# Paired attentions: the inverse sums, copied 64 wide, are turned by TensorE, and ScalarE's copies stand between its exponentials

## The reference, cut to what matters

```python
def gqa_attend(q, k, v, bias=None, sink=None):
    s = einsum("bqhgd,bkhd->bhgqk", q, k) * ATTN_SCALE
    if bias is not None: s = s + bias
    if sink is not None:
        p = softmax(concatenate([s, sink_col], axis=-1), axis=-1)[..., :-1]
    else:
        p = softmax(s, axis=-1)
    return einsum("bhgqk,bkhd->bqhgd", p, v)
```

## Time and profile before

| what | value |
|---|---|
| timed runs | 1794.65, 1794.69, 1797.04 us |
| the profiled execution's own time | 1799.19 us |
| its span in the profile | 1797.9 us |
| PE, DVE, ACT, POOL busy | 96%, 55%, 41%, 36% of the span |
| even attention, first scores to last output | about 1138 to 1336 us |
| odd attention, first scores to last output | about 1614 to 1691 us |

### The profile page before, as it was taken

One profiled execution on the slowest core, in us unless ns is written; L12 is line 12 of the kernel. 1 busy time (PEld: TensorE's weight loads), 2 busy tenths in 40 slices (PEclk: granted clock), 3 DMA queues, 4 the chain that ended last, 5 costly groups with the idle time before them and its releaser, 6 DMA issues.

```text
span 1797.9 us, 24836 instructions
## 1 busy us (share of the span) xinstructions
PE 1724.9 (96%) x9530; PEld 1386.2 (77%) x9530; DVE 990.7 (55%) x2000; ACT 742.1 (41%) x1465; POOL 641.6 (36%) x272
## 2 busy tenths in 40 slices
PE   8999999889999999999999999999889999999997
PEld 6889666678888888888788876655568888896776
DVE  4797545533233455555792415566643667975553
ACT  5222344552333454344324432466753225225553
POOL 3877222253334454544646122100003233521132
PEclk9999999999999999999999999999999999999999
DMA  8656221132324233333662221100002442321021
GB/s 236 188 141 188 65 71 48 48 98 80 93 70 141 82 89 99 94 94 99 187 194 88 66 90 36 36 1 1 2 1 59 134 127 74 88 68 47 14 89 53
DMA packets 255155, 156.30 MB, mean 87 GB/s; under 512 B 6017, under 2 KB 250942, under 8 KB 255038
## 3 DMA queue, kind: packets, MB, share of 16 engines
q1 hardware_dynamic: 251518, 147.12, 28.1%
q10 hardware_dynamic: 3520, 7.60, 1.2%
HBM read 152.60 MB, written 2.10 MB: 86 GB/s over the span
## 4 chain that ended last, share of the span: by engine, by line
PE 83%; DVE 7%; issue 4%; ACT 3%; POOL 1%; DMA 1%; ACTq 0%; DVEq 0%; SPq 0%
PE ps L783 66%; PE ps L2417 3%; PE ps L2428 2%; PE ps L2447 2%; POOL w_lo L764 1%; PE ps L1567 1%; DVE mod_sums L1500 1%; PE ps L1551 1%; PE ps L1515 1%; DVE mod_sums_odd L1500 1%; DVE probs L2519 1%; PE ps L789 1%; PE ps L1559 1%; PE ps L2453 1%; PE ps L2165 1%
## 5 line engine op out<-in xcount | busy, mean ns | idle before, releaser
L764 POOL TENSOR_TENSOR w_lo<-w_raw,w_hi 128x1024 fp32r<-128x1024 f32 (+1 forms) x220 | 586.2, 2669 | 1080.9 <-ACT w_hi L705 1080.4
L783 PE MATMUL ps<-h_hi,w_lo 128*128 128x512 f32 x1088 | 433.6, 399 | 10.5 <-DVE h_lo L1102 2.9
L783 PE MATMUL ps<-h_hi,w_hi 128*128 128x512 f32 x1088 | 424.5, 390 | 0.0
L783 PE MATMUL ps<-h_lo,w_hi 128*128 128x512 f32 x1088 | 424.2, 390 | 0.0
L783 PEld LDWEIGHTS ps<-h_hi,w_lo 128*128 128x128 f32 x1088 | 204.5, 188 | 59.8 <-issue 6.0
L705 ACT ACTIVATE w_hi<-w_raw 128x1024 fp32r<-128x1024 f32 (+1 forms) x220 | 228.6, 1044 | 37.1 <-PE ps L783 20.6
L783 PEld LDWEIGHTS ps<-h_hi,w_hi 128*128 128x128 f32 x1088 | 204.3, 188 | 43.7
L783 PEld LDWEIGHTS ps<-h_lo,w_hi 128*128 128x128 f32 x1088 | 204.6, 188 | 41.2 <-issue 1.4
L2502 ACT ACTIVATE probs<-probs,small 128x512 f32<-128x512 f32 (+3 forms) x128 | 93.7, 732 | 24.0 <-DVE small L2519 21.2
L2428 PE MATMUL ps<-ident,probs 128*128 128x128 f32 x528 | 85.8, 287 | 15.2 <-ACT probsT L2485 7.0
L2428 PEld LDWEIGHTS ps<-ident,probs 128*128 128x128 f32 x528 | 56.5, 142 | 54.4 <-issue 30.3
(11 more groups left out here) (425 smaller groups left out, 3313.6 us busy)
## 6 DMA issues: line engine op xcount, KB each, us to landing
w_raw<-in_w_in SPq DMA_DIRECT2D x56, 512.0 KB, 5.2
mod_raw<-in_mod_w SPq DMA_DIRECT2D x24, 1024.0 KB, 5.9
w_raw<-in_w_up SPq DMA_DIRECT2D x44, 512.0 KB, 3.8
w_raw<-in_od_w_in SPq DMA_DIRECT2D x28, 512.0 KB, 3.8
w_raw<-in_ev_w_in SPq DMA_DIRECT2D x20, 512.0 KB, 3.8
w_raw<-in_w_down SPq DMA_DIRECT2D x16, 512.0 KB, 4.3
w_raw<-in_w_mem_kv SPq DMA_DIRECT2D x8, 512.0 KB, 3.9
w_raw<-in_w_attn_branch SPq DMA_DIRECT2D x8, 512.0 KB, 4.0
```

What stands on the lines that cost most here:

```text
L764: POOL.tensor_tensor(wlo[:, p, 0:n], raw[:, p, 0:n], f(whi[:, p, 0:n]), ALU.subtract).then_inc(*chunk_lo.by(c))
L783: ins = PE.matmul(out, l, r, start=first and n == 0, stop=last and n == 2)
```

## The change: what it does

- The inverse sums are no longer spread by four matmuls for each output. VectorE copies the 128x2x2 inverses of an output 64 times over into a new buffer inv_wide (128x2x128, one buffer) in a new function `dve_widen`, once for each output: in steps p = 2g+3, behind the output of that step and ahead of the first head's maximum. It waits for the reciprocal of the output's second pair and for `p_weighted` of the output before. TensorE turns the two 128x128 halves of inv_wide with two transposes in the same place of its order and waits for the new event `p_widened` there.
- VectorE's reciprocal no longer waits for `p_weighted`.
- ScalarE's order in step p is now: first head's copy of pair p-1, first head's exponential of pair p, in even steps p = 2g+4 the inverse of output g, second head's copy of pair p-1, second head's exponential of pair p.
- The events `conv_summed` and `ln_summed` become two events of one semaphore; no instruction is added or removed by it.

```diff
--- before.py
+++ after.py
@@ -189,6 +189,7 @@
     stat = sb("statistics", [P, len(NORMS) + 2, 8])
     rowvec = sb("rowvec", [1, 16])
     djunk = nc.alloc_sbuf_tensor_at("diff_squares", [P, 2, P], F32, offset=base[0])
+    inv_wide = nc.alloc_sbuf_tensor_at("inv_wide", [P, 2, P], F32, offset=base[0])
     lamrow = sb("lamrow", [1, 4, DIFF_DH])
     modT = sb("mod_T", [P, 2, 24, 2])
     R0 = base[0]
@@ -490,6 +491,7 @@
     p_copied_act = signal("p_copied_act", halves)
     p_inverted = signal("p_inverted", pairs)
     p_weighted = signal("p_weighted", outs)
+    p_widened = signal("p_widened", outs)
     p_inv_copied = signal("p_inv_copied", outs)
     p_attended = signal("p_attended", outs)
 
@@ -552,12 +554,11 @@
     g_lo = signal("g_lo", gated + each("cg", 4))
     glu_done = signal("glu_done", range(4))
     convolved = signal("convolved", range(CT))
-    conv_summed = signal("conv_summed", [0])
+    conv_summed = signal("conv_summed", ["values", "squares"])
     mean_set = signal("mean_set", [0])
     centred = signal("centred", range(CT))
     bias_masked = signal("bias_masked", range(8))
     ln_squared = signal("ln_squared", range(CT))
-    ln_summed = signal("ln_summed", [0])
     ln_rms = signal("ln_rms", [0])
     ln_diag = signal("ln_diag", [0])
     ln_spread = signal("ln_spread", [0])
@@ -2446,12 +2447,9 @@
             for s in range(2):
                 PE.matmul(ps[s * HEAD:(s + 1) * HEAD, b * 512 + lo:b * 512 + hi], u0["v"](k, s),
                           probsT[s][g % 2][:, k, lo:hi], start=n == 0, stop=n == len(tiles) - 1, skip_group_check=True)
-        PE.wait_ge(*p_inverted(x_, 2 * g + 1))
+        PE.wait_ge(*p_widened(x_, g))
         for n in range(2):
-            inv = pair_stats(2 * g + n)[2]
-            for s in range(2):
-                ins = PE.matmul(ps[s * HEAD:(s + 1) * HEAD, b * 512 + (2 + n) * P:b * 512 + (3 + n) * P],
-                                inv[:, s:s + 1].to_broadcast([P, HEAD]), ident[:])
+            ins = PE.transpose(bank(b, P, (2 + n) * P), inv_wide[:, n, :], ident[:])
         ins.then_inc(*p_weighted.by(x_, g))
         yield
 
@@ -2486,15 +2484,19 @@
                             ACT.Copy).then_inc(*p_copied_act.by(x_, p, s))
 
         for p in range(n + 3):
-            if p >= 5 and p % 2:
-                act_inverse((p - 5) // 2, x_, us)
             if 1 <= p <= n:
                 copy(p - 1, 0)
+            if p > n and p % 2 == 0:
+                act_inverse((p - 4) // 2, x_, us)
             if p < n:
                 u = us[p]
                 neg_max, total, _, esink = pair_stats(p)
                 before(p)
                 for s in range(2):
+                    if s and p >= 4 and p % 2 == 0:
+                        act_inverse((p - 4) // 2, x_, us)
+                    if s and p:
+                        copy(p - 1, 1)
                     ACTE.wait_ge(*p_maxed(x_, p, s))
                     if p >= 4:
                         ACTE.wait_ge(*p_inverted(x_, p - 4))
@@ -2503,10 +2505,10 @@
                     if "sink" in u:
                         ins = ACTE.activation(esink[:, s:s + 1], u["sink"][s], ACT.Exp, bias=neg_max[:, s:s + 1])
                     ins.then_inc(*p_exped.by(x_, p, s))
-            if 1 <= p <= n:
+            if p == n:
+                act_inverse((p - 4) // 2, x_, us)
                 copy(p - 1, 1)
             yield
-        act_inverse(n // 2 - 1, x_, us)
 
     def dve_maximum(x_, p, u, s, probs):
 
@@ -2534,6 +2536,8 @@
         for p in range(n + 3):
             if p >= 5 and p % 2:
                 dve_out((p - 5) // 2, x_, us)
+            if 3 <= p <= n + 1 and p % 2:
+                dve_widen((p - 3) // 2, x_)
             if p < n:
                 before(p)
                 dve_maximum(x_, p, us[p], 0, probs)
@@ -2542,8 +2546,6 @@
                 u = us[p - 1]
                 _, total, inv, esink = pair_stats(p - 1)
                 DVE.wait_ge(*p_exped(x_, p - 1, 1))
-                if p >= 5:
-                    DVE.wait_ge(*p_weighted(x_, (p - 5) // 2))
                 if "sink" in u:
                     dve_step(DVE.tensor_tensor(total, total, esink, ALU.add))
                     dve_after()
@@ -2554,6 +2556,16 @@
                 copy(p - 1, 1)
             yield
         dve_out(n // 2 - 1, x_, us)
+
+    def dve_widen(g, x_):
+
+        DVE.wait_ge(*p_inverted(x_, 2 * g + 1))
+        if g:
+            DVE.wait_ge(*p_weighted(x_, g - 1))
+        at = 48 + 16 * (g % 2)
+        inv = small[:, at:at + 16].rearrange("p (n e) -> p n e", n=2)[:, :, 4:6]
+        DVE.tensor_copy(inv_wide[:].rearrange("p n (s d) -> p n s d", s=2),
+                        inv.unsqueeze(3).to_broadcast([P, 2, 2, HEAD])).then_inc(*p_widened.by(x_, g))
 
     def dve_out(g, x_, us):
 
@@ -3009,17 +3021,17 @@
             for t in range(CT):
                 PE.wait_ge(*convolved(t))
                 ins = PE.matmul(bank(1), ones[:], yc[:, t, :], start=t == 0, stop=t == CT - 1)
-            ins.then_inc(*conv_summed.by(0))
+            ins.then_inc(*conv_summed.by("values"))
         if p == 9:
             for t in range(CT):
                 PE.wait_ge(*ln_squared(t))
                 for b in range(NB):
                     ins = PE.matmul(bank(3, 1, b), sqc[t][:, b * P:(b + 1) * P], ones[:, 0:1], start=t == 0 and b == 0,
                                     stop=t == CT - 1, skip_group_check=True)
-            ins.then_inc(*ln_summed.by(0))
+            ins.then_inc(*conv_summed.by("squares"))
 
     def act_ln_mean():
-        ACTE.wait_ge(*conv_summed(0))
+        ACTE.wait_ge(*conv_summed("values"))
         ACTE.activation(mean[:], bank(1), ACT.Copy, scale=1.0 / 512).then_inc(*mean_set.by(0))
 
     def dve_ln_centre(t):
@@ -3033,7 +3045,7 @@
 
     def act_ln_root():
         ACTE.preload_act_table(ACT.Sqrt)
-        ACTE.wait_ge(*ln_summed(0))
+        ACTE.wait_ge(*conv_summed("squares"))
         ACTE.activation(statistics("ln")[0], bank(3, NB), ACT.Sqrt, scale=1.0 / 512, bias=eps).then_inc(*ln_rms.by(0))
         ACTE.preload_act_table(ACT.Exp)
 
```

## The result

The changed kernel's median is 1787.26 us (1785.91 to 1788.40, 5 executions), against 1796.99 us of the kernel before in its 5. The ratio is 0.995, with a 95% interval of 0.9935 to 0.9964: it is 6.5 to 11.7 us faster. 1787.26 lies inside the range, but the 14 us of the forecast lie outside the interval. The profiled execution took 1788.40 us, span 1787.1.

What follows compares the result with a forecast made beforehand. PE was taken to bound the kernel (83% of the chain), idling 22.8 us in three attention stretches. Terms 7.7 + 6.8 + 1.6 - 1.5 - 0.5 = 14.1, taken as 14, gave a median of 1780.7 us, range 1776.5 to 1788.

Steps and rivals of the forecast that it cites:

- part 1: PE, all 32 outputs: two transposes replace the four inverse matmuls, saving 0.24 us each, 7.7 us in all.
- part 5: In B, PE's scores wait longer for the second maximum: about half of 12 outputs return their 0.24, 1.5 us.
- the clock as a rival: Two-tile pairs of A and B: transposes make PE's clock fall, 3.4 us each; six falls give 1801 us; chance 0.03.
- Parts 2 and 3: ACT's second copy ahead of its second exponential saves 6.8 us; ACT's inverse one step earlier saves 1.6 in B.
- Part 4: DVE's widening copy, 32 times 0.35 us, 11 us in all, is hidden by the wait for the inverse it replaces.
- The rival of the uncovered copy: DVE's widening copy delays the maxima and costs PE 0.2 us per output, 32 outputs; gain 7.6 us, 1787.1; chance 0.14.
- 0.5 for the start: Steps at each attention's very start run beside the last projections and lack these stalls: 0.5 us off the gain.
- the 4 us that I had named as the mark of an error: Sign of being wrong: PE's wait in B for DVE's maxima (L2519) grows past 4 us.
- the 1.9 forecast for ACT's stalls: In A, PE's 3 waits for ACT's copy, 1.9 us, go; counted within the 6.8 us for ACT's second copy.
- The rival in which everything comes back: ACT's stalls return as waits for DVE's copies and maxima; gain only 2 to 4 us, about 1792; chance 0.07.

Runs made afterwards that it cites:

- the copy alone: Kernel before with only ScalarE's second copy moved ahead of its second exponential; ratio 0.9991, 2.5 us less in the attentions.
- the inverse alone: Kernel before with only ScalarE's copy of the inverse moved from step 2g+5 to 2g+4, between the exponentials; ratio 0.9979, 2.7 us less in the attentions.
- the order alone: Changed kernel with the four inverse matmuls and VectorE's wait for `p_weighted` back, no widening copy, ScalarE's new order kept; ratio 0.9958.

## Why the prediction was right and wrong

The mechanism was the one forecast: the waits for ACT's copy vanished, DVE found its inverse ready in B, the widening copy was hidden, and what was late next was the second maximum. The size was too big by 4 us, 14 against 9.9. It failed in two steps: the gain of the attentions was carried over to the whole program one to one, which left out the clock (2.0 us), and the sum for the attentions was 14.1 where they gave 12.4, mostly in part 1 and in what comes back of it (part 5). Some 0.5 us are left unexplained.

- **What stood outside the sum: the clock, 2.0 us.** I carried the gain in the attentions over to the whole program one to one. I had the clock as a rival only in the two-tile pairs, on the ground of the transposes. There it didn't come: B kept 1.00 in every profile, and A had one fall of 3.4 us near 1155 us before and after alike. The rule of the Trainium skill, "TensorE: Matmul & The Clock Gate", section "Part 4: PE-mode transpose", that transposes don't count as busy for the clock as other matmuls do, is thus not borne out in B, where 176 transposes and 24 new ones changed nothing. It is a test only of turns with scores and values between them. The falls that made the difference were elsewhere; why they come there no run here shows.
- **Part 1, the inverses, 7.7 us: 7.0 by its price, 4.3 in the end.** From the start of the values over the inverses and the turn of six to the next scores it took 1188.38 - 1185.69 = 2.69 us before, and 1190.48 - 1188.01 = 2.47 in the changed kernel. That is 0.22 saved per output, not 0.24. Up to the start of the turn it is only 1.89 - 1.72 = 0.17; the turn itself then takes 0.05 less behind two transposes than behind the four matmuls. I had priced the two as two more in a run; by this count they are 0.02 dearer. The scores of the kernel before, and the stretch of the changed kernel:

```profile
1188.38 0.48 PE L2417 MATMUL ps<-k_A,q_A 64*128 64x256 f32 x1
```

```profile
1188.01 1.51 PE L2448 MATMUL ps<-probsT,v_A 128*64 128x256 f32 x12
1189.46 0.44 PE L2452 MATMUL ps<-ident,inv_wide 128*128 128x128 f32 x2
1189.73 0.82 PE L2429 MATMUL ps<-ident,probs 128*128 128x128 f32 x6
1190.48 0.48 PE L2418 MATMUL ps<-k_A,q_A 64*128 64x256 f32 x1
```

  On top of the new order this part gave 12.4 - 8.1 = 4.3 us, so 2.7 of the 7.0 came back; see part 5. Without the new order it gave nothing in A and came out 1.3 us slower in B.
- **Parts 2 and 3, the order, 6.8 + 1.6: 8.1 together.** Right as a pair, wrong as terms: 2.5 for the copy alone, 2.7 for the inverse alone. So it was partly luck that the two terms added up to nearly the right sum. Each removed wait uncovers the other within a few tenths of a microsecond.
- **Part 4, the copy, 0.35 us and hidden:** the median is 0.28 us (0.31 in the mean, for one copy in the odd attention took 1.04), the next instruction begins 0.20 behind its start, and it is hidden in A and B. Right but for that one: the step that holds it takes 4.27 us, against 3.84 with the order alone. The rival of the uncovered copy, 0.2 us of PE for each of 32, is out.
- **Part 5, what is late next, 1.5 us back, and 0.5 for the start:** 2.7 came back. In seven steps of B that hold an output's inverses nothing of the 0.22 is left, 1.5 us, as forecast. I had left out three such steps of A that keep only 0.09, where scores that had come right behind the turn now wait 0.04 for the maximum (0.4 us), the one long copy (0.4), the last outputs of B and of the odd attention (0.4), and 0.1 at the start of A. In B the wait for the maxima grew from 1.9 to 4.3 us, that is 2.4, of which 0.8 came with the order alone. Right in kind and place; it crossed the 4 us that I had named as the mark of an error, and moving 0.34 us of VectorE's work out of this line gave 3.8 us more in B.

A gave 3.5 us and not 5: the order 1.8, near the 1.9 forecast for ACT's stalls, and the inverses 1.7, from the ten outputs of its window, of which three gave only 0.09. The odd attention gave 1.8 us, corrected for its clock, against 2. The rival in which everything comes back is out as well: of PE's 6.8 us of waits for copies in B 5.5 went, and 2.4 came back as waits for the maxima. With the base too I was a little off: the median of three, 1794.69, is 2.1 below the mean of 63.

## What to carry to other kernels

Where several engines pass tiles round in a loop, a wait in the profile is worth its length only until the next event arrives, so add up waits only after going through the loop with all the moves in place. Look in each in-order queue for an instruction that stands ahead of what another engine needs and that nobody needs soon: here an exponential, an inverse and a reciprocal. And when gains of half a per cent are judged, read the changed stretch by its own borders, which repeated to 0.1 us where whole executions of one kernel scattered by 5 us or more.

## What the hardware showed that I had not expected

Executions of one and the same kernel differ, and with them how much PE's clock falls: 63 of the kernel before ranged from 1791.2 to 1803.1 us, at a mean granted clock from 0.994 to 0.987, and over all kernels 0.001 went with 1.38 us. Removing PE's work made the kernel slower when it stood alone: with 128 float32 matmuls gone and 64 transposes and 32 copies of DVE in their place, the ratio was 1.0017. A copy of 256 elements a partition, read from SBUF columns 64 times over, took 0.28 us in the median on DVE with its successor 0.20 us behind, faster than the 0.42 of a copy of that size from PSUM. But it was held up whenever it began beside an instruction of GpSimd (here always the masking of the odd attention's bias), as in the changed kernel:

```profile
1635.46 3.59 POOL L3003 TENSOR_TENSOR bias<-bias,near_mask 128x768 f32<-128x768 f32 x2 [18.20 <-DMA bias<-in_rpb_rows]
...
1638.16 1.04 DVE L2567 COPY inv_wide<-small 128x256 f32<-128x256 f32 x1
```

GpSimd ends at 1639.05 and the copy 0.15 us later. All twelve widening copies that began beside a GpSimd instruction, over the eight profiles of kernels that have them, ended 0.15 us behind it and took 0.33 to 1.19 us.
